# ScalarE builds one batch's weighted one-hots, and the last stage takes its data from on-chip memory, in a hybrid layer with product-key experts

## The reference, cut to what matters

```
m = SiLU(cond) @ w_mod + b_mod                # shifts, scales and gates of both sub-layers
h = rmsnorm(x) * (1 + scale_mix) + shift_mix
q, k, v, x_rg, y_rg = split(h @ w_in)         # 1024 -> 2560
A = attention(q, k, v)                        # latent: 8x16 window, bias, and all context keys
B = (scan_fwd + scan_bwd)(conv(x_rg)) * gelu(y_rg)      # gated linear recurrences
x = x + gate_mix * (concat(A, B) @ w_out)
h = rmsnorm(x) * (1 + scale_ffn) + shift_ffn
# experts: 8 heads, two halves of 128 keys each, the 16 best of 16 x 16 pairs of keys
e, g = top16(h @ w_q, sub_keys), softmax      # e = first * 128 + second
x = x + gate_ffn * sum_e g_e * gelu(h . u[e]) * v[e]
y = rmsnorm(x, norm_f)
```

## Time and profile before

| | |
|---|---|
| median of 3 runs | 3778.87 us (3778.69 to 3785.31) |
| profiled execution, its own time | 3790.08 us |
| its span (first to last event) | 3788.3 us |
| mean granted TensorE clock | 0.921 |
| busy: PE | 3158.0 us (83%) |
| busy: PEld | 2086.8 us (55%) |
| busy: DVE | 2639.1 us (70%) |
| busy: ACT | 1044.5 us (28%) |
| busy: POOL | 1958.1 us (52%) |
| DMA traffic | 1137.21 MB, mean 300 GB/s |

### The profile page before, as it was taken

One profiled execution on the slowest core, in us unless ns is written; L12 is line 12 of the kernel. 1 busy time (PEld: TensorE's weight loads), 2 busy tenths in 40 slices (PEclk: granted clock), 3 DMA queues, 4 the chain that ended last, 5 costly groups with the idle time before them and its releaser, 6 DMA issues. The chain is left out here.

```text
span 3788.3 us, 47442 instructions
## 1 busy us (share of the span) xinstructions
PE 3158.0 (83%) x15281; PEld 2086.8 (55%) x15281; DVE 2639.1 (70%) x5952; ACT 1044.5 (28%) x1812; POOL 1958.1 (52%) x1772
## 2 busy tenths in 40 slices
PE   5677599789869889377477899998999999999992
PEld 4446244556434333267455667676676766766662
DVE  2126678688374786999577778787787787875445
ACT  4441043366111010266211222222222222222111
POOL 0001455445245887322366677776777677775550
PEclk9788799899889999688789999999999999999996
DMA  6522487766578997258899999999999999999996
GB/s 246 188 89 96 161 268 242 218 213 219 195 249 284 318 336 262 95 167 250 272 388 370 350 407 408 403 406 381 408 403 408 385 405 400 408 405 362 352 343 247
DMA packets 412551, 1137.21 MB, mean 300 GB/s; under 512 B 33992, under 2 KB 129480, under 8 KB 412160
## 3 DMA queue, kind: packets, MB, share of 16 engines
q0 software_dynamic: 221184, 805.40, 57.1%
q1 hardware_dynamic: 191232, 330.14, 24.2%
HBM read 1079.60 MB, written 55.81 MB: 300 GB/s over the span
## 5 line engine op out<-in xcount | busy, mean ns | idle before, releaser
L2253 POOL DMA_INDIRECT exp_value_row<-in_v_rows,exp_v_id x568 | 711.9, 1253 | 273.5 <-issue 177.7
L2300 DVE CUSTOM_DVE_ANT_0 edge_row<-edge_row,edge_x 128x1024 f32<-128x1024 f32 x480 | 583.5, 1218 | 277.5 <-DMA edge_row<-in_u_rows,edge_u_id 242.9
L2245 POOL DMA_INDIRECT edge_row<-in_u_rows,edge_u_id x480 | 511.1, 1065 | 354.0 <-DVE edge_dot L2300 204.8
L375 POOL DMA_INDIRECT ahead_row<-in_u_rows,keep_expert_id x256 | 327.0, 1277 | 372.9 <-DVE keep_dot L385 310.3
L2134 PE MATMUL exp_a_ps<-exp_xT_hi,exp_u_hi 128*128 128x512 f32 x1024 | 410.3, 401 | 41.0 <-DVE exp_u_lo L2269 31.4
L2149 PE MATMUL exp_o_ps<-exp_v_hi,exp_w_hi 128*128 128x512 f32 x1024 | 338.0, 412 | 83.6 <-DVE keep_acc L2364 83.3
L2134 PE MATMUL exp_a_ps<-exp_xT_lo,exp_u_hi 128*128 128x512 f32 x1024 | 401.6, 392 | 0.0
L2134 PE MATMUL exp_a_ps<-exp_xT_hi,exp_u_lo 128*128 128x512 f32 x1024 | 401.2, 392 | 0.0
L2364 DVE TENSOR_TENSOR keep_acc<-exp_o_ps,keep_acc 128x1024 f32<-128x1024 f32 x256 | 311.4, 1220 | 108.1 <-PE exp_o_ps L2149 107.4
L385 DVE CUSTOM_DVE_ANT_0 ahead_row<-ahead_row,ahead_x 128x1024 f32<-128x1024 f32 x256 | 304.5, 1220 | 79.0 <-DMA ahead_row<-in_u_rows,keep_expert_id 75.3
L2149 PE MATMUL exp_o_ps<-exp_v_lo,exp_w_hi 128*128 128x512 f32 x1024 | 324.2, 398 | 0.0
(11 more groups left out here) (373 smaller groups left out, 5132.2 us busy)
## 6 DMA issues: line engine op xcount, KB each, us to landing
edge_u_raw<-in_uT SPq DMA_DIRECT2D x130, 512.0 KB, 6.7
exp_v_raw<-in_v_rows SPq DMA_DIRECT2D x128, 512.0 KB, 6.7
exp_g_raw<-scratch_g SPq DMA_DIRECT2D x128, 256.0 KB, 6.5
scratch_g<-place_grid SPq DMA_DIRECT2D x3, 8192.0 KB, 35.8
proj_ctx_mod_slab<-in_w_mod SPq DMA_DIRECT2D x8, 2048.0 KB, 14.4
proj_ctx_slab<-in_w_in SPq DMA_DIRECT2D x10, 1024.0 KB, 5.2
proj_lat_slab<-in_w_in SPq DMA_DIRECT2D x10, 1024.0 KB, 11.4
exp_value_row<-in_v_rows,exp_v_id POOLq DMA_INDIRECT x568, 7.8
```

The lines of the kernel that those rows point to most:

```text
L375: nc.gpsimd.indirect_dma_start(out=ahead.row[:, n % KEY_RING, :], out_offset=None, in_=io["u_rows"], in_offset=bass.IndirectOffsetOnAxis(a ...
L2245: nc.gpsimd.indirect_dma_start(out=key_row[:, j % RING, :], out_offset=None, in_=io["u_rows"], in_offset=bass.IndirectOffsetOnAxis(ap=u_id ...
L2253: nc.gpsimd.indirect_dma_start(out=value_row[:, 4 * (j % 2) + t, :], out_offset=None, in_=io["v_rows"].rearrange("a b n -> (a b) n"), in_o ...
L2300: nc.vector.tensor_tensor_reduce(out=key_row[:, j % RING, :], in0=key_row[:, j % RING, :], in1=x, scale=1.0, scalar=0.0, op0=ALU.mult, op1 ...
```

## The change

Placing. Batch 2 (`MADE_BY_ACT`) is made in another way. DVE makes only its column one-hots (128x512). ACT makes the weighted row one-hots from the iota: `Square(iota - first)`, then `Relu(weight - weight * square)`, which is the weight where the key is met and, the weights being positive, zero at every other whole number. The negated first keys and weights are made once into `minus`. Four Squares, a wait of ACT for its own results (`squared`), and four Relus stand where four scaled copies stood; PE waits for the column one-hots as well. The second store of the last tile's grid is issued by ACT.

Latent projection and attention. The first two slab halves are loaded by SP at the end of the context routing into a buffer of its own (`Early.room`), which attention's `probT` later shares. `k_ctxT` is loaded in the projection stage, behind `rg_cols`, into the fourth part of `acc`.

Latent routing. One step of the gathered values' work on PE (`factor_turn`) comes behind the first group of projection products instead of before it.

Experts and last norm. `acc` is no longer stored; the last norm reads tiles 0 to 3 from it. In the first round behind number `LAST` (57) five loads of 512 KB bring `x1` of tiles 0 to 2, the latent gate and `norm_f`. The last norm works tile by tile with a ring of four output buffers, and POOL multiplies tiles 4 to 7 by the gate.

The diff, cut to its core:

```diff
+class Early:
+    def __init__(self, scope, signals, k_ctx):
+        self.room = scope.sb("room", [P, 2 * KD * SLAB // 2])
+        self.slab = [self.room[:, n * KD * SLAB // 2:(n + 1) * KD * SLAB // 2].rearrange("p (k n) -> p k n", k=KD)
+                     for n in range(2)]
+        self.k_ctx = k_ctx
+        self.slab_in = [signals.sem(f"{scope.stage}_slab_in{n}") for n in range(2)]
+        self.k_in = signals.sem(f"{scope.stage}_k_in")
+def load_half(io, sp, early, a, n):
+    HALF = SLAB // 2
+    sp.dma_start(early.slab[n], io["w_in"].rearrange("(j p) n -> p j n", p=P)[:, :, a * SLAB + n * HALF:a * SLAB + (n + 1) * HALF])\
+      .then_inc(early.slab_in[n], 16)
...
-            load_half(0, 0)
+            if context:
+                load_half(io, sp, early, 0, 0)
             sp.dma_start(cols[:, 0:RG_ROWS, :], io["rg_cols"]).then_inc(cols_in, 16)
-            load_half(0, 1)
+            if context:
+                load_half(io, sp, early, 0, 1)
+            else:
+                sp.dma_start(early.k_ctx, io["k_ctxT"]).then_inc(early.k_in, 16)
             load_weights(0)
...
                 sp.dma_start(slab[:, a % 2, :, :], w_q[:, :, a * SLAB:(a + 1) * SLAB]).then_inc(slab_in[a % 2], 16)
+            if early:
+                for n in range(2):
+                    load_half(io, sp, early, 0, n)
...
-            if val:
-                factor_turn(nc, keep, val, pe, 0, h_ps)
...
                         last.then_inc(q_made, 1)
+                        if val and turn == 0:
+                            factor_turn(nc, keep, val, pe, 0, h_ps)
...
-    SCALED_BY_ACT, SCALED_BY_DVE = (0, 2), (1, 3)
+    SCALED_BY_ACT, SCALED_BY_DVE, MADE_BY_ACT = (0, 2), (1, 3), 2
...
+            for t in range(DENSE_TILES):
+                mine_by_act = cols[:, t, 0:3:2, :].rearrange("p n (m s) -> p n m s", s=STEP)\
+                    [:, :, :, MADE_BY_ACT * BATCH:(MADE_BY_ACT + 1) * BATCH]
+                last = nc.vector.tensor_scalar(minus[:, t, :, :].rearrange("p n (m s) -> p n m s", s=BATCH),
+                                               mine_by_act, -1.0, None, ALU.mult)
+            last.then_inc(minus_ready, 1)
...
+                    if b == MADE_BY_ACT:
+                        nc.vector.tensor_tensor(
+                            hot[:, b, 1, :, :], keep["iota"][:, :].unsqueeze(1).broadcast_to([P, BATCH, N_KEYS]),
+                            cols[:, t, 1, at:at + BATCH].unsqueeze(2).broadcast_to([P, BATCH, N_KEYS]), ALU.is_equal)\
+                          .then_inc(hot_ready, 1)
+                    elif b in SCALED_BY_ACT:
...
                         pe.wait_ge(scaled, 2 * before + SCALED_BY_ACT.index(b) + 1)
+                        if b == MADE_BY_ACT:
+                            pe.wait_ge(hot_ready, 2 * before + SCALED_BY_ACT.index(b) + 1)
...
+                    if b == MADE_BY_ACT:
+                        if before == 0:
+                            act.wait_ge(minus_ready, 1)
+                        else:
+                            act.wait_ge(made, BATCHES * (before - 1) + b + 1)
+                        for k in range(BATCH):
+                            last = nc.scalar.activation(hot[:, b, 0, k, :], keep["iota"][:, :], ACT.Square,
+                                                        bias=minus[:, t, 0, m * BATCH + k:m * BATCH + k + 1])
+                        last.then_inc(squared, 1)
+                        act.wait_ge(squared, before + 1)
+                        for k in range(BATCH):
+                            last = nc.scalar.activation(hot[:, b, 0, k, :], hot[:, b, 0, k, :], ACT.Relu,
+                                                        scale=minus[:, t, 1, m * BATCH + k:m * BATCH + k + 1],
+                                                        bias=cols[:, t, 2, at + k:at + k + 1])
+                        last.then_inc(scaled, 1)
+                        continue
...
+            act.wait_ge(placed, DENSE_TILES * PER_TILE)
+            nc.scalar.dma_start(scratch["g"].rearrange("b a t -> a b t")[:, FIRST_KEYS:N_KEYS, (DENSE_TILES - 1) * P:DENSE_TILES * P],
+                                grid[1][:, FIRST_KEYS:N_KEYS, :]).then_inc(edge.g_rest, 16)
...
-            sp.dma_start(place[:, FIRST_KEYS:N_KEYS, last], grid[1][:, FIRST_KEYS:N_KEYS, :]).then_inc(edge.g_rest, 16)
...
+                if mode == "values" and isinstance(r, int) and r == LAST + 1:
+                    sp.wait_ge(dots, SLOTS * LATENT_GATHER + RING)
+                    load_early(io, scratch, ahead, edge, sp)
...
-            sp.wait_ge(added, DENSE_TILES * (ROUNDS + 1))
-            sp.dma_start(scratch["ffn"][0:DENSE_TILES].rearrange("t p n -> p t n"), acc[:, :, :]).then_inc(acc_out, 16)
-            sp.wait_ge(acc_out, 16)
...
+EARLY_TILES = 3
+def load_early(io, scratch, ahead, edge, sp):
+    for t in range(EARLY_TILES):
+        sp.dma_start(ahead.row[:, t, :], scratch["x1"][t]).then_inc(edge.early_in, 16)
+    sp.dma_start(ahead.row[:, EARLY_TILES, :], scratch["gate"][:, LATENT_COND, :]).then_inc(edge.early_in, 16)
+    sp.dma_start(ahead.x[:, 0, :], io["norm_f"].partition_broadcast(P)).then_inc(edge.early_in, 16)
+def final_norm(nc, io, keep, scratch, ahead, edge):
+    RING = 4
+    LATE = range(DENSE_TILES, TILES)
+    BY_POOL = (4, 5, 6, 7)
...
+        def dense(t):
+            return keep["acc"][:, t, :] if t < DENSE_TILES else f[:, t, :]
+        def mixed(t):
+            return ahead.row[:, t, :] if t < EARLY_TILES else x1[:, t, :]
         @block.sync
         def _(sp):
-            sp.dma_start(gate[:, :, :], scratch["gate"]).then_inc(w_in, 16)
-            sp.dma_start(norm_w[:, :], io["norm_f"].partition_broadcast(P)).then_inc(w_in, 16)
-            for i in range(PAIRS):
-                for source, out in (("ffn", f), ("x1", x1)):
-                    sp.dma_start(out[:, 2 * i:2 * i + 2, :], scratch[source][2 * i:2 * i + 2].rearrange("t p n -> p t n"))\
-                      .then_inc(pair_in[i], 16)
+            sp.dma_start(x1[:, EARLY_TILES, :], scratch["x1"][EARLY_TILES]).then_inc(x1_in, 16)
+            for t in LATE:
+                if t == LATENT_TILES:
+                    sp.dma_start(gate[1], scratch["gate"][:, CONTEXT_COND, :]).then_inc(gate_in, 16)
+                sp.dma_start(f[:, t, :], scratch["ffn"][t]).then_inc(late_in[t - DENSE_TILES], 16)
+                sp.dma_start(x1[:, t, :], scratch["x1"][t]).then_inc(late_in[t - DENSE_TILES], 16)
             for t in range(TILES):
                 sp.wait_ge(y_ready, t + 1)
-                sp.dma_start(io["y"][t * P:(t + 1) * P, :], y[:, t % 2, :]).then_inc(y_out[t % 2], 16)
-            for j in range(2):
-                sp.wait_ge(y_out[j], 16 * PAIRS)
+                sp.dma_start(io["y"][t * P:(t + 1) * P, :], y[:, t % RING, :]).then_inc(y_out[t % RING], 16)
+            for j in range(RING):
+                sp.wait_ge(y_out[j], 16 * len(range(j, TILES, RING)))
+        @block.gpsimd
+        def _(pool):
+            pool.wait_ge(edge.early_in, 16 * (EARLY_TILES + 2))
+            for t in BY_POOL:
+                pool.wait_ge(late_in[t - DENSE_TILES], 32)
+                nc.gpsimd.tensor_tensor(f[:, t, :], f[:, t, :], gate[0], ALU.mult).then_inc(gated_pool, 1)
...
+            dve.wait_ge(edge.early_in, 16 * (EARLY_TILES + 2))
+            marks = itertools.count(1)
+
+            def residual(t):
+                if t >= LATENT_TILES:
+                    dve.wait_ge(gate_in, 16)
+                if t == EARLY_TILES:
+                    dve.wait_ge(x1_in, 16)
+                if t >= DENSE_TILES:
+                    dve.wait_ge(late_in[t - DENSE_TILES], 32)
+                if t in BY_POOL:
+                    dve.wait_ge(gated_pool, BY_POOL.index(t) + 1)
+                else:
+                    nc.vector.tensor_tensor(dense(t), dense(t), gate[0 if t < LATENT_TILES else 1], ALU.mult)\
+                      .then_inc(gated, 1)
+                    dve.wait_ge(gated, next(marks))
+                nc.vector.tensor_tensor(dense(t), dense(t), mixed(t), ALU.add).then_inc(x2_ready, 1)
...
+            residual(1)
+            for t in range(TILES):
+                if t + 2 < TILES:
+                    residual(t + 2)
+                dve.wait_ge(root_ready, t + 1)
+                nc.vector.reciprocal(rstd[:, t:t + 1], total[:, t:t + 1]).then_inc(rstd_ready, 1)
+                dve.wait_ge(rstd_ready, t + 1)
+                if t >= RING:
+                    dve.wait_ge(y_out[t % RING], 16 * (t // RING))
+                nc.vector.scalar_tensor_tensor(y[:, t % RING, :], dense(t), rstd[:, t:t + 1], norm_w, ALU.mult, ALU.mult)\
```

105 lines of the change are left out of this document (42 added, 63 removed).

## The result

| | before | after |
|---|---|---|
| median | 3778.87 us (5 runs, 3768.97 to 3785.31) | 3747.07 us (5 runs, 3734.33 to 3754.10) |
| ratio | | 0.9903, 95% interval 0.9882 to 0.9924 |
| span of the profiled execution | 3788.3 us | 3745.3 us |
| mean granted TensorE clock | 0.921 | 0.936 |

The changed kernel is 32 us faster by the two medians, and 37 us by the ratio (28.7 to 44.6 by its interval). The two profiled executions lie 43 us apart; some 8 us of that are not the change's doing (experiment 2).

What follows compares the result with a forecast made beforehand. The prediction held that no engine bounds the whole span and priced each stretch separately: +3 − 8 − 2 + 0 + 4 − 17 = −20 us, from 3778.9 to 3759 us, range 3739 to 3773 (forecast's own 3750 to 3769).

Steps and rivals of the forecast that it cites:

- Placing, +3: Placing: the longer ACT-PE chain makes a step 6.93 us on average instead of 6.84, 3 us slower in all.
- the slower PE time: Placing: PE's 5.46 us a step, 1.62 more, leaves a step at 6.88 us, or at most 7.36.
- rival D: Placing: PE, idling twice a step, stays at 1.2 GHz; +76 us in all, 3832 us; chance 0.05.
- Latent projection, −8: Start of the latent projection: earlier slab loads let PE start about 10 us earlier, of which 8 us are gained.
- PE may have to give a part back: Latent projection: DVE's lag may return as a PE wait, leaving 6 us of the 10 gained.
- Attention, −2, at most −3: Attention: one 512 KB load less ahead of the bias loads, 1.3 us at 407 GB/s, 2 with its issue.
- Experts, +4: Experts: five early loads, 2.6 MB, cost 6.4 us of full DMA engines, partly made up later; 4 us slower.
- Latent routing, 0: Latent routing: the factor step moved behind the first projection products changes nothing, as PE waits for the first slab anyway.
- The end, −17: Last stage: no accumulator store and an earlier start, less DVE blocked by POOL; 17 us faster.
- the 2 us of other waits: Last stage: 2 us allowed for DVE waits other than the 9.4 us blocked by POOL.
- The sums of the ends: Whole kernel: the terms' best and worst cases added up, −53 and −1 us, both at once called unlikely.
- A: Whole kernel: no POOL-DVE blocking, early loads free, projection's head gains its 10 us; −36 us, 3743 us; chance 0.15.

Runs made afterwards that it cites:

- experiment 2: Kernel before with only the changed placing stage put in; ratio to before 1.0005 (0.9979 to 1.0031).
- experiment 9: Kernel before with placing's 32 dot products on DVE cut from 1024 to 64 columns; placing's copies span 216.0 us.
- experiment 4: Changed kernel with ACT scaling the next step's batch 0 ahead of the copies of batches 2 and 3; ratio to before 0.9871.
- experiment 11: Changed kernel with the first two slab halves loaded at the latent projection's head again; head 10.9 us, projection 305.0 us.
- experiment 8: Changed kernel with the k_ctx load back at attention's head; 22.5 us from the projection's last product to the bias addition.
- e6: Kernel before with ACT scaling the next step's batch 0 ahead of the copies of batches 2 and 3; ratio to before 0.9989.

## Why the prediction was right, and where it was off

In the latent projection, the experts and the end the mechanism was as forecast; in placing the reason given was wrong, and in attention the price. The sum was 12 us short by the medians and 17 by the ratio. From the distances, without the 7.7 us that are not the change's, −10.1 − 6.5 − 1.9 + 3.8 − 20.9 = −35.6, against −31.8 of the medians and −36.7 of the ratio, whose interval is 8 us on either side.

- *Placing, +3.* Measured −1 (−1.9 in this pair). The step at the full clock was 6.75 against 6.88, because the wait for ACT's own result costs 0.03 us here, not the 0.17 of the earlier trace rows (why the two differ stays open). And the slower PE time hardly came with it: the clock was 0.94 to 0.98 in the seven traces. The prediction put no clock above the 0.82 of before into its sum, and named the idle time cut in two only as a point against rival D; that the clock rose so far is luck. The prediction said that the price of the longer chain is small only because DVE's 6.74 stood beside it. That reason was wrong (experiment 9: DVE did not bind). The price was small because the clock gave back what the chain cost. Two slips stand in the working. The stretch of 215.00 us holds 31.4 steps of 6.84, not 31, so DVE's work was 6.65 a step and PE's 5.0, which is what makes 1.85 + 5.0 = 6.84; DVE's 6.65 less 0.53 is 6.12, close to the step of 6.14 that experiment 4 reached. And a PE slower by 1.62 on batches 0 and 1 does not fit in the 1.2 it idles: such a step would be 7.3, not 6.88.
- *Latent projection, −8.* Measured −10.1. The step that failed is "PE may have to give a part back": it gave back nothing (experiment 11).
- *Attention, −2, at most −3.* Measured −6. The step that failed priced the load at 407 GB/s. Beside the gathers SP's queue moved 103 (experiment 8), and by that rate the load is 5 us; this explanation is argued, the 6 us are measured.
- *Experts, +4.* Measured +3.8 in the round of the loads, and not given back later.
- *Latent routing, 0.* Not resolved: the distance that holds it scatters by 7 us.
- *The end, −17.* Measured −20.9. DVE did stand still beside POOL, 4 × 2 us: four instructions of 3.17 to 3.36 instead of 1.22 to 1.28 make 8.0, where 9.4 was taken; the 2 us of other waits did not come (between its first product and its last instruction DVE idles 0.6 us), and the stage began 1.6 us after the last addition began, not 2. The 37.59 us of DVE's work also held 1.0 us of the experts' last addition, which ends at 3723.0.

The terms that were mis-sized most are placing (by 4 or 5), the end (4) and attention (4), then the projection (2). All erred to the same side. In the projection and at the end a piece had been taken that would come back as a new wait, and it did not. The sums of the ends are −51 and 0, where −53 and −1 stand; the range did not hang on it. Of the rivals, D (the low clock) went the other way, and A's sum was nearer the median than the forecast's, but not by A's mechanism: POOL and DVE do block each other, and the early loads do cost the experts 3.8 us.

## What to carry to other kernels

An engine that is busy 97% of a stage need not be its bound: a chain of two others with a gap in it can be as long, and shortening the busy one then gains nothing until the order in the chain is changed (here 1 us without, 16 with). Work moved to GpSimd can cost VectorE more than it takes from it: here each moved product of 1.22 us held up a VectorE instruction with two inputs in SBUF for 2.0. And a small load at the head of a stage is to be priced at the rate that its queue gets beside the others there, not at the best rate of the DMA engines.

## What the runs showed of the hardware that I had not expected

- The granted clock did not follow the sum of PE's idle time. In placing, with 57 us of waits in single gaps of 1.85 a step, it was 0.82 in three traces; with 80 us, in two gaps of 1.85 and 0.80, it was 0.94 to 0.98 in seven; with 63 us in gaps of 1.76 and 0.28 it was 1.00 in two; with 67 us in gaps of changing length up to 1.9 (e6) it was 0.93. These are means of the two levels that it takes, 1.2 and 2.4 GHz. The Trainium skill's page "TensorE: Matmul & The Clock Gate", section "What's actually happening", treats the clock as released by activity; here the stage with more idle time had the higher clock. Which feature of the pattern decides, the runs do not tell.
- GpSimd and VectorE hold each other up both ways: POOL's product of 128x1024 took 3.18 us on average in the last stage instead of 2.34, each of the four beside one VectorE instruction of 3.2 to 3.4 us. Moving the products back to VectorE gained 2.9 us. This agrees with the Trainium skill's page "SBUF — State Buffer", section "Who interferes with whom".
